# Expert tiles take turns in eight rooms; the router's weights and the first gather come earlier

## The chip, the cores and the metric

The kernel runs on one core of one Trainium2 chip. The time is the device time of one execution in microseconds. The reference takes one sequence of 256 tokens, 1024 features wide, all in float32.

## What is computed

The reference is a three-layer model; the change touches the second half of its first layer, the mixture of experts:

```python
x = x + g1[:, None, :] * y
h2 = modulate(x, norm2_g[l], sh2, sc2)
moe = hier_moe(h2.reshape(b * s, d), w_rg[l], b_rg[l], w_re[l], b_re[l],
               w1[l], w3[l], w2[l]).reshape(b, s, d)
x = x + g2[:, None, :] * moe
...
gp = softmax(h @ w_rg + b_rg);          g_w, g_idx = top_k(gp, 1)
el = (h @ w_re + b_re).reshape(t, 4, 8) # the 8 experts of the chosen group
e_w, e_loc = top_k(softmax(el_sel), 2)
weights = g_w * e_w / sum(e_w)
ys = (silu(xb @ w1[e]) * (xb @ w3[e])) @ w2[e]
```

There are 32 experts; a token goes to two of them. An expert has three weight tiles of [128 x 4096] float32 (2048 KB each): two with w1 and w3, one with w2. So 96 expert tiles are read whatever the routing. The layers behind it need the keys and values of a memory (256 rows by the matrices `w_kv`), which are computed in pieces beside the experts.

## The kernel before

Work is split in stages, each a block with one instruction stream per engine and a barrier of all engines at its end. All weights are read by SP, on one DMA queue, in the order in which SP issues them; SP waits on semaphores between the issues.

`stage_mix` (line 313) does attention, the recurrent mixer and the out projection. It streams the weight tiles named in `FRONT` through a ring of three slots, `ring`: tile n goes to slot n % 3 and is issued when tile n - 3 has been used (`tile(n)`, line 382). Between ring tiles SP also loads expert tiles that have buffers of their own: `expert0_0`, `expert0_1`, `expert0_2` for expert 0 (lines 406 to 414; the last two wait until the mixer no longer uses these buffers), and `early`, the first tile of expert 2. O0 and O1 are the two tiles of the out projection (PE line 560), A0 to A11 those of the adaptive modulation (line 287), M2 a tile of memory values kept in `mem_tile`. At the end of the stage PE turns the normed x by tokens (line 567), and DVE and ACT modulate it into `hT` (lines 998, 1006), the first half of the tokens in this stage, the second in the next.

`stage_route` (line 1029) loads the router's weights and bias row, the three ring slots with the tiles of expert 1, and two quarters of memory weights (`mem_part`, 512 KB each). PE computes the logits (line 1070), turns them and h back to tokens (lines 1086, 1076), does modulation tile A11 and, when DVE has chosen the experts, five small matmuls for the ranks (lines 1091 to 1095). DVE makes the combination weights while it waits for these. SP loads the row of the last norm (`norm_f`, line 1063) and waits for it before it leaves the stage.

`stage_experts` (line 1195) holds the accumulators in PSUM and goes through 16 pairs of experts. Each engine first reads the number of passes (here one). DVE makes the selection matrices for a pair (`select_pair`) and the weighted ones; PE gathers the tokens of a pair (`gather`, line 1286), DVE copies them to `x_gathered`. For an expert PE multiplies with tiles 0 and 1 (line 1339), does a piece of the memory's keys or values where one falls due (lines 1311, 1316), turns the weighted selection, scatters the expert before (line 1297), and multiplies with tile 2 (line 1364). Even experts use the `expert0` buffers, odd ones the ring's three slots; SP reloads a buffer when the tile in it has been used (line 1244), so seven tiles at most are in or on their way. A memory quarter is reloaded after both tiles and the last multiply of its expert. The pairs are in five code bodies: pairs 0 and 1 alone, 2 and 3, 4 to 7 and 8 to 15 as loops:

```python
SEGMENTS = ((0, 1, ("first", "keys0")), (1, 1, ("first", "keys0")), (2, 2, ("first", "keys0")),
            (4, 4, ("keys0", "keys1")), (8, 8, ("values", None)))
```

`stage_first_end` (line 1469) adds the result to x and norms it; the next layer (`tail`) streams its weights through the same ring.

## Time and profile before

| | us |
|---|---|
| median of 3 runs | 1506.67 (1505.97 to 1508.27) |
| the profiled execution | 1507.86 |
| its span | 1506.1 |
| PE busy | 1375.8 (91%) |
| PE's weight loads | 1042.6 (69%) |
| DVE, ACT, POOL busy | 656.4, 263.5, 229.2 |
| moved by DMA | 387.74 MB, mean 257 GB/s |

The stages in the profiled execution: the mixer to 221 us, the router to 247, the experts to 733, the rest behind.
### The profile page before, as it was taken

To read this page: it belongs to the slowest core of one execution; us is meant where nothing else is said; L and a number is where in the kernel's file an instruction comes from. 1 tells how busy PE (TensorE), PEld (TensorE's weight loads), DVE (VectorE), ACT (ScalarE), POOL (GpSimd) and SP (SyncE) were. 2 spreads that over 40 slices of the span, in tenths; PEclk is the share of its full clock that TensorE was granted. 3 is DMA by queue.
4 is the path that set the end of the run, shared out by engine and by line. 5 is a ranking of instruction groups with operands and counts; after the bars stand their busy time and mean duration, and the time that the engine had idled before them with its cause. 6 is when DMAs were issued, how large, how long until landed. Compare 5 with 4: busy or idle time off the path is not lost. (4 is left out here: it accounts for less than half of the span.)

```text
span 1506.1 us, 24580 instructions
## 1 busy us (share of the span) xinstructions
PE 1375.8 (91%) x10107; PEld 1042.6 (69%) x10107; DVE 656.4 (44%) x1235; ACT 263.5 (17%) x570; POOL 229.2 (15%) x227
## 2 busy tenths in 40 slices
PE   5999877998888888877899999999999999899998
PEld 2475434776556565555568788888887887788887
DVE  2545432111001110101353317376299999886573
ACT  2212111111101101100211022100233333330000
POOL 0000100000000000000166450099322122000000
PEclk9999996999989989988999999999999999999999
DMA  9637855999999999999743343556564444334441
GB/s 396 239 132 280 359 195 209 416 427 427 428 428 430 427 429 428 429 428 429 287 160 139 112 154 126 194 183 221 180 216 143 157 163 155 129 112 159 154 174 45
DMA packets 50797, 387.74 MB, mean 257 GB/s; under 512 B 6288, under 2 KB 21392, under 8 KB 29088
## 3 DMA queue, kind: packets, MB, share of 16 engines
q1 hardware_dynamic: 48128, 381.35, 64.0%
q10 hardware_dynamic: 2592, 5.31, 1.0%
q8 instruction: 54, 0.88, 0.2%
q14 instruction: 23, 0.19, 0.0%
HBM read 379.76 MB, written 6.88 MB: 257 GB/s over the span
## 5 line engine op out<-in xcount | busy, mean ns | idle before, releaser
L2551 PE MATMUL ps<-hT,ring 128*128 128x256 f32 x768 | 169.9, 381 | 1.0 <-PEq L1991 1.0
L2551 PEld LDWEIGHTS ps<-hT,ring 128*128 128x128 f32 x768 | 145.7, 192 | 20.3 <-issue 1.4
L1461 DVE TENSOR_TENSOR act_slots<-gate,ps 64x256 f32<-64x256 f32 x32 | 13.5, 423 | 241.0 <-ACT gate L1395 241.0
L1339 PE MATMUL ps<-expert,x_gathered 128*32 128x256 f32 x1024 | 72.4, 439 | 22.5 <-DMA expert<-in_experts 21.5
L1528 POOL TENSOR_SCALAR end_stat<-end_ss 128x1 f32<-128x1 f32 x2 | 0.9, 473 | 515.0 <-ACT expert L1518 514.9
L1339 PEld LDWEIGHTS ps<-expert,x_gathered 128*32 128x32 f32 x1024 | 36.2, 125 | 54.3 <-DMA expert<-in_experts 25.5
L1311 PE MATMUL ps<-memT,mem_part 128*128 128x256 f32 x192 | 53.7, 442 | 20.6 <-DMA mem_part<-in_mem_quarters 20.6
L267 PE MATMUL ps<-ring,hT 128*128 128x512 f32 x160 | 69.8, 594 | 0.0
L1286 PEld LDWEIGHTS ps<-sel,tokens 128*128 128x128 f32 x544 | 65.9, 200 | 5.0 <-issue 3.3
L1286 PE MATMUL ps<-sel,tokens 128*128 128x64 f32 x544 | 66.8, 284 | 0.4 <-DVE sel_weighted L1438 0.4
L1840 PE MATMUL ps<-ring,zT 128*128 128x256 f32 x288 | 66.9, 380 | 0.0
L1311 PEld LDWEIGHTS ps<-memT,mem_part 128*128 128x128 f32 x192 | 41.9, 224 | 32.9 <-DMA mem_part<-in_mem_quarters 23.9
L1339 PE MATMUL ps<-ring,x_gathered 128*32 128x256 f32 x1024 | 59.0, 380 | 2.0 <-DMA ring<-in_experts 2.0
L1840 PEld LDWEIGHTS ps<-ring,zT 128*128 128x128 f32 x288 | 54.6, 190 | 7.2
L1316 PE MATMUL ps<-mem_part,memT 128*128 128x128 f32 x256 | 42.0, 342 | 18.6 <-DMA mem_part<-in_mem_quarters 18.6
L1316 PEld LDWEIGHTS ps<-mem_part,memT 128*128 128x128 f32 x256 | 40.5, 253 | 23.9 <-DMA mem_part<-in_mem_quarters 23.9
L1463 DVE COPY x_gathered<-ps 128x512 f32<-128x512 f32 x16 | 11.1, 692 | 103.3 <-PE ps L1286 103.3
L2034 PE MATMUL ps<-hT,ring 128*128 128x256 f32 x256 | 55.7, 379 | 0.0
L267 PEld LDWEIGHTS ps<-ring,hT 128*128 128x128 f32 x160 | 30.0, 190 | 35.8 <-issue 35.8
L2659 POOL TENSOR_TENSOR ab_tmp<-b_raw,s_a_rows 128x256 f32<-128x256 f32 x32 | 28.0, 896 | 164.7 <-PE ps L2566 110.3
L2034 PEld LDWEIGHTS ps<-hT,ring 128*128 128x128 f32 x256 | 48.6, 190 | 6.4
L1438 DVE TENSOR_SCALAR sel_weighted<-const,rank,comb 128x128 f32<-128x128 f32 x66 | 19.9, 344 | 73.8 <-PE ps L1292 72.2
(651 smaller groups left out, 2523.0 us busy)
## 6 DMA issues: line engine op xcount, KB each, us to landing
ring<-in_weights SPq DMA_DIRECT2D x69, 2048.0 KB, 8.1
expert<-in_experts SPq DMA_DIRECT2D x48, 2048.0 KB, 22.3
ring<-in_experts SPq DMA_DIRECT2D x48, 2048.0 KB, 25.0
mem_part<-in_mem_quarters SPq DMA_DIRECT2D x20, 512.0 KB, 20.5
s_c_bar<-c_bar_out ACTq DMA_DIRECT2D x16, 256.0 KB, 2.4
c_bar<-s_c_bar SPq DMA_DIRECT2D x16, 256.0 KB, 2.7
mem_tile<-in_weights SPq DMA_DIRECT2D x1, 2048.0 KB, 21.7
b_raw<-in_s_b SPq DMA_DIRECT2D x16, 128.0 KB, 7.2
```

Source lines behind the costliest of these rows:

```text
L267: last = pe.matmul(bank, src[:, kk, h * P:(h + 1) * P], w[:, kk, :], start=(kk == 0), stop=(kk == KD - 1))
L1286: last = pe.matmul(xg_ps[:, f, :], a["tokens"][:, t, f * P:(f + 1) * P], sel[:, t].rearrange("p e s -> p (e s)"), start=(t == 0), stop=(t ...
L1311: last = pe.matmul(out, w[:, kk, :], k.memT[:, kk, :], start=(kk == 0), stop=(kk == KD - 1))
L1316: last = pe.matmul(out[:, h * P:(h + 1) * P], k.memT[:, kk, h * P:(h + 1) * P], cols, start=(kk == 0), stop=(kk == KD - 1))
L1339: last = pe.matmul(h_ps[group(g), :], xg[:, f, group(b)], w[:, kk, g, :], start=(f == 0), stop=(f == KD - 1))
L1438: last = dve.tensor_scalar(selw[:, b, t, :], k.c("iota32"), a["rank"][:, t, e], a["comb"][:, t, e], ALU.is_equal, ALU.mult)
L1461: dve.tensor_tensor(act_s[:], gate[:], h_ps[w3_out, :], ALU.mult).then_inc(act_ready, 1)
L1463: dve.tensor_copy(xg[:], xg_ps).then_inc(xg_ready, 1)
L1840: last = pe.matmul(self.sum_of(n, p), rows[:, kk, :], w[:, kk, :], start=(first and kk == 0 and self.PLACE[p][1] == 0), stop=(self.ends(i) ...
L2034: last = pe.matmul(bank[:, f, :], w[:, kk, (2 * h + f) * P:(2 * h + f + 1) * P], k.hT[:, kk, :], start=(kk == 0), stop=(kk == KD - 1))
L2551: last = pe.matmul(out[:, f, :], w[:, kk, (2 * h + f) * P:(2 * h + f + 1) * P], k.hT[:, kk, :], start=(kk == 0), stop=(kk == KD - 1))
L2659: pool.tensor_tensor(t_ab[:, c], b, bc(a_fm[:, q % 2, c, :], 1, 2), ALU.mult)
```

## The change

Expert tiles are numbered 0 to 95. Tile 0 goes to a room of its own, the buffer in which the memory's keys and values (`kmT`, `vm`) are put later; the others take turns in eight rooms. Tile n is issued when tile n - 8 has been used, in order. The eight are the three `expert0` buffers, one that was `early`, the three ring slots, and a new one, `late_room`, that exists from the router's stage on. Space comes from the memory quarters, which now go to `hT`, from the last norm's row, which goes to the row of `b_g1`, from the gate tiles, which go to `ada_part`, and from the mixer's `gate_quads` and `a_rows`, which go to a part of `expert0_1`.

```diff
+def room_of(k, a, n):
+    return [a["expert0"][0][:], a["room"][:], a["expert0"][1][:], a["expert0"][2][:], k.ring[:, 2, :], k.ring[:, 0, :],
+            a["late_room"][:] if "late_room" in a else None, k.ring[:, 1, :]][(n - 1) % N_ROOM] if n else a["kv"]
+
+def load_expert_tile(k, sp, a, n):
+    sp.dma_start(room_of(k, a, n), k.dram["experts"][n]).then_inc(room_landed(a, n), 16)
...
+                sp.dma_start(a["w_router"][:], d["w_router"]).then_inc(a["w_router_in"], 16)
+                at = ROWS["b_router"][0]
+                sp.dma_start(a["b_router"][:], d["rows"][at:at + 36].partition_broadcast(P)).then_inc(a["b_router_in"], 16)
                 for n in range(7, TILE_OF["A11"] + 1):
                     tile(n)
-                    if n == TILE_OF["VM"]:
-                        load_early(k, sp, a)
-                    if n == TILE_OF["A7"]:
-                        load_expert(k, sp, a, 0, 0)
-                    if n == TILE_OF["A9"]:
+                    if 7 <= n < 10:
+                        load_expert_tile(k, sp, a, n - 7)
+                    if n == TILE_OF["O0"]:
                         sp.wait_ge(pv_done, 4)
                         sp.wait_ge(silu_done, 2)
-                        load_expert(k, sp, a, 0, 1)
+                        sp.wait_ge(a_bc, 1)
+                        load_expert_tile(k, sp, a, 3)
                     if n == TILE_OF["A10"]:
                         sp.wait_ge(squares, 2)
-                        load_expert(k, sp, a, 0, 2)
+                        load_expert_tile(k, sp, a, 4)
...
                 turn_x(1)
+                pe.wait_ge(a["w_router_in"], 16)
+                pe.wait_ge(h_first_ready, 2)
+                logits_of(k, a, pe, 0)
```

The router's stage, SP:

```diff
-                sp.dma_start(w_router[:], k.dram["w_router"]).then_inc(router_in, 16)
-                at = ROWS["b_router"][0]
-                sp.dma_start(b_router[:], k.dram["rows"][at:at + 36].partition_broadcast(P)).then_inc(router_in, 16)
-                load_expert(k, sp, a, 1, TILE_OF["O1"] % RING)
-                load_expert(k, sp, a, 1, TILE_OF["A10"] % RING)
-                for b in range(2):
-                    load_part(k, sp, a, b, N_KEYS0 // 2 * (1 - b))
+                load_expert_tile(k, sp, a, 6)
+                load_expert_tile(k, sp, a, 7)
                 sp.wait_ge(k.tile_done, TILE_OF["A11"] + 1)
-                load_expert(k, sp, a, 1, TILE_OF["A11"] % RING)
+                load_expert_tile(k, sp, a, 5)
+                sp.wait_ge(h_turned, TT)
+                load_part(k, sp, a, 1)
+                load_expert_tile(k, sp, a, 8)
+                load_part(k, sp, a, 8)
                 at = ROWS["norm_f_g"][0]
-                sp.dma_start(a["norm_f"][:], k.dram["rows"][at:at + D].partition_broadcast(P)).then_inc(norm_f_in, 16)
-                sp.wait_ge(norm_f_in, 16)
+                sp.dma_start(a["norm_f"], k.dram["rows"][at:at + D].partition_broadcast(P)).then_inc(a["norm_f_in"], 16)
```

DVE waits for `norm_f_in` at the head of `stage_first_end` instead. In the router's stage ACT takes A11's part before it copies h; DVE computes ranks and `passes` first, then `select_pair`, then the combination weights and the late row of G11:

```diff
+                dve.drain()
+                select_pair(k, a, dve, lambda e: slice(e, e + 1)).then_inc(first_sel_ready, 1)
+                dve.wait_ge(exp_done, 1)
```

In the experts' stage SP is written out for all tiles, PE for twelve pairs (pairs 0 to 7, and a body of four that is gone through twice), and a memory quarter is reloaded after the first two tiles of its expert:

```diff
+                    for q in range(N_PAIR):
+                        for b in range(2):
+                            for j in range(3):
+                                load_next(p, 6 * q + 3 * b + j)
+                                if j == 1 and KINDS[q // 4][b] is not None:
+                                    load_next_part(p, part_of(q, b))
...
+                    for q0 in (0, 4):
+                        for r in range(4):
+                            pair(p, 0, q0 + r, KINDS[q0 // 4])
+                    with pe.Fori(0, 2) as i:
+                        for r in range(4):
+                            pair(p, i, 8 + r, KINDS[2])
...
-                for n in (T_END_FIRST, T_END_FIRST + 2, T_END_FIRST + 1):
-                    sp.wait_ge(done, n_pass * (3 * N_EXP) + (n % RING + 1 - 3 + DONE0))
+                for n, last in ((T_END_FIRST, 88), (T_END_FIRST + 1, 93), (T_END_FIRST + 2, 94)):
+                    sp.wait_ge(done, n_pass * N_TILE + (last + 1 - N_TILE + DONE0))
```

SP's issues in the second half of the mixer's stage, before (`ring` from `in_weights` are ring tiles 7 to 20, `in_experts` is the source of the expert tiles; `expert_0` is `early` the first time and `expert0_0` the second, since numbers inside a name are cut):

```order
L385 DMA ring<-in_weights 128x4096 x5
L1026 DMA expert_0<-in_experts 128x4096
L385 DMA ring<-in_weights 128x4096 x3
L1014 DMA expert_0<-in_experts 128x4096
L385 DMA ring<-in_weights 128x4096 x2
L1014 DMA expert_1<-in_experts 128x4096
L385 DMA ring<-in_weights 128x4096 x3
L1014 DMA expert_2<-in_experts 128x4096
L415 DMA mem_tile<-in_weights 128x4096
L385 DMA ring<-in_weights 128x4096
```

and now (from the router's weights on):

```order
L402 DMA w_router<-in_w_router 128x288
L404 DMA b_router<-in_rows 128x36
L385 DMA ring<-in_weights 128x4096
L1029 DMA kv<-in_experts 128x4096
L385 DMA ring<-in_weights 128x4096
L1029 DMA expert_0<-in_experts 128x4096
L385 DMA ring<-in_weights 128x4096
L1029 DMA expert_room<-in_experts 128x4096
L385 DMA ring<-in_weights 128x4096 x8
L1029 DMA expert_1<-in_experts 128x4096
L385 DMA ring<-in_weights 128x4096 x2
L1029 DMA expert_2<-in_experts 128x4096
```

Expert tiles 0, 1 and 2 now follow ring tiles 7, 8 and 9; `expert_1` is loaded after O0 (ring tile 17), where it was loaded before it, and the router's weights lead.

PE at the barrier between the mixer's stage and the router's (`UNCONDITIONAL_BRANCH` marks a stage's end and the next one's begin), before:

```order
L310 MATMUL ps<-ada_part,const 128x512
L567 MATMUL ps<-const,tokens 128x128 x8
L379 UNCONDITIONAL_BRANCH
L1066 UNCONDITIONAL_BRANCH
L1070 MATMUL ps<-hT,w_router 36x128 x16
L1076 MATMUL ps<-const,hT 128x128 x8
L1086 MATMUL ps<-const,logits_turned 128x36 x2
L1076 MATMUL ps<-const,hT 128x128 x8
```

and now:

```order
L310 MATMUL ps<-ada_part,const 128x512
L569 MATMUL ps<-const,tokens 128x128 x8
L1048 MATMUL ps<-hT,w_router 36x128 x8
L379 UNCONDITIONAL_BRANCH
L1112 UNCONDITIONAL_BRANCH
L287 MATMUL ps<-ring,crep 32x512 x8
L1048 MATMUL ps<-hT,w_router 36x128 x8
L1116 MATMUL ps<-const,hT 128x128 x8
```

Half of the logits (L1048, once L1070) stand ahead of the barrier now, and tile A11 (L287) stands ahead of the other half.

PE at the barrier between the router's stage and the experts', before:

```order
L1095 MATMUL ps<-chosen,const 128x32
L310 MATMUL ps<-ada_part,const 128x512
L1050 UNCONDITIONAL_BRANCH
L1279 UNCONDITIONAL_BRANCH
L1234 TENSOR_LOAD passes
L1234 ISA x2
L1372 MATMUL ps<-y,selT 128x512 x4
L1286 MATMUL ps<-sel,tokens 128x64 x16
```

and now:

```order
L1133 MATMUL ps<-chosen,const 128x32
L1134 MATMUL ps<-chosen,const 128x32
L1057 MATMUL ps<-sel,tokens 128x64 x16
L1098 UNCONDITIONAL_BRANCH
L1316 UNCONDITIONAL_BRANCH
L1276 TENSOR_LOAD passes
L1276 ISA x2
L1405 MATMUL ps<-y,selT 128x512 x4
```

The gather (L1057, once L1286) stands ahead of the barrier and of the load of `passes`; it stood behind them.

## Rows read from the trace of the kernel before

**Rows 1.** The page, the span in 40 slices of 37.65 us: GB/s.
```profile
GB/s 396 239 132 280 359 195 209 416 427 427 428 428 430 427 429 428 429 428 429 287 160 139 112 154 126 194 183 221 180 216 143 157 163 155 129 112 159 154 174 45
```

**Rows 2.** Stretches: length, busy us of each engine, granted clock, DMA share, GB/s.
```profile
201.00:212.00 11.00, 11.00 (x26) 4.96 (x27) 3.26 (x5) 1.44 (x4) 0.99 (x3) 1.00 0.01 1
...
246.00:262.00 16.00, 12.90 (x88) 9.41 (x92) 3.08 (x10) 1.28 (x1) 0.00 (x0) 0.52 0.04 8
...
282.00:726.00 444.00, 381.06 (x4465) 265.88 (x4464) 49.11 (x164) 47.94 (x141) 0.00 (x0) 0.92 1.00 425
```

**Rows 3.** Waits of PE, 255 to 780 us: sum, times, longest.
```profile
PE ps L1339 <- DMA expert<-in_experts: 21.5, 8, 3.0
PE ps L1311 <- DMA mem_part<-in_mem_quarters: 20.6, 5, 4.2
PE ps L1316 <- DMA mem_part<-in_mem_quarters: 18.6, 7, 2.8
...
PE ps L1339 <- DMA ring<-in_experts: 2.0, 4, 0.6
...
PE ps L1547 <- PEq L1236: 0.3, 1, 0.3
```

**Rows 4.** PE in order of time, third and fourth expert: start, length, instructions.
```profile
284.45 3.64 PE L1339 MATMUL ps<-expert,x_gathered 128*32 128x256 f32 x64
...
302.43 3.68 PE L1286 MATMUL ps<-sel,tokens 128*128 128x64 f32 x32
...
309.57 3.64 PE L1339 MATMUL ps<-expert,x_gathered 128*32 128x256 f32 x64
```

**Rows 5.** DMA in 255 to 275, 275 to 700, 700 to 760, 205 to 255.
```profile
expert<-in_experts SPq DMA_DIRECT2D x3, 2048.0 KB, 9.9
...
q8 instruction: 11, 0.18, 0.2%
...
ring<-in_experts SPq DMA_DIRECT2D x1, 2048.0 KB, 25.0
...
ring<-in_weights SPq DMA_DIRECT2D x1, 2048.0 KB, 8.1
...
norm_f<-in_rows SPq DMA_DIRECT2D x1, 512.0 KB, 9.2
```

**Rows 6.** PE in order of time around the out projection.
```profile
181.45 16.42 PE L560 MATMUL ps<-ring,mix_room 128*128 128x512 f32 x32 [4.55 <-DMA ring<-in_weights]
...
200.90 14.00 PE L560 MATMUL ps<-ring,mix_room 128*128 128x512 f32 x32 [1.32 <-DVE mix_room L968]
```

**Rows 7.** In order of time, router and first expert: one row of ACT, then PE.
```profile
221.38 1.50 ACT L998 ACTIVATE hT<-ps,mod 128x128 f32<-128x128 f32 x4 [2.35 <-PEq L379]
...
227.38 5.31 PE L1070 MATMUL ps<-hT,w_router 128*36 128x128 f32 x32 [6.30 <-DMA b_router<-in_rows]
...
239.45 0.41 PE L1091 MATMUL ps<-chosen,const 128*128 128x32 f32 x2 [2.62 <-DVE chosen L1163]
...
247.76 1.04 PE L1372 MATMUL ps<-y,selT 64*128 64x512 bf16 x4 [5.50 <-PEq L1050]
249.17 7.09 PE L1286 MATMUL ps<-sel,tokens 128*128 128x64 f32 x32 [0.37 <-DVE sel_weighted L1438]
257.23 5.73 PE L1339 MATMUL ps<-expert,x_gathered 128*32 128x256 f32 x64 [0.97 <-DVE x_gathered L1449]
```

**Rows 8.** SP's longest wait for a landing, 215 to 260, and two of its issues.
```profile
SPq L1050 <- DMA norm_f<-in_rows: 8.7, 1, 8.7
...
237.27 0.43 SPq L1063 DMA_DIRECT2D norm_f<-in_rows  x1
260.93 9.82 SPq L1244 DMA_DIRECT2D expert<-in_experts  x3
```

**Rows 9.** DVE in order of time, end of the router, start of the experts.
```profile
242.34 0.15 DVE L1192 TENSOR_SCALAR passes<-most 128x1 int32<-128x1 f32 x1
247.93 0.68 DVE L1432 TENSOR_SCALAR sel<-const,rank 128x32 f32<-128x32 f32 x4 [5.43 <-issue]
```

More of the change, by code:

```diff
@@ L518, in _ @@
                 for h in range(4):
-                    last = pe.matmul(abc[:, h, :], k.c("one_hot4")[0:4, h * P:(h + 1) * P], a_rows[:], start=True, stop=True)
+                    last = pe.matmul(abc[:, h, :], k.c("one_hot4")[0:4, h * P:(h + 1) * P], a_rows, start=True, stop=True)
                 last.then_inc(a_bc, 1)
@@ new lines, in logits_of, with gather @@
+def logits_of(k, a, pe, t):
+    for kk in range(KD):
+        last = pe.matmul(a["by_expert_ps"][:, t * P:(t + 1) * P], a["w_router"][:, kk, :], k.hT[:, kk, t * P:(t + 1) * P],
+                         start=(kk == 0), stop=(kk == KD - 1))
+    return last
+def gather(k, a, pe):
+    for f in range(KD):
+        for t in range(TT):
+            last = pe.matmul(a["xg_ps"][:, f, :], a["tokens"][:, t, f * P:(f + 1) * P],
+                             a["sel"][:, t].rearrange("p e s -> p (e s)"), start=(t == 0), stop=(t == TT - 1))
+    last.then_inc(a["xg_done"], 1)
@@ L1105, in _ @@
                 act_modulate(k, a, act, 1).then_inc(h_ready, 1)
+                act.wait_ge(*banks.full("A11"))
+                act.activation(a["part"][:], banks.bank("A11"), ACT.Copy).then_inc(banks.out("A11"), 1)
                 for t in range(TT):
@@ L1108, in _ @@
                     act.copy(h[:, t, :], a["turned_x"](t).rearrange("p f e -> p (f e)")).then_inc(h_copied, 1)
-                act.wait_ge(*banks.full("A11"))
-                act.activation(a["part"][:], banks.bank("A11"), ACT.Copy).then_inc(banks.out("A11"), 1)
                 act.wait_ge(gap_ready, 1)
@@ L1217, in stage_experts @@
         part_ps = k.ps[:, 7, TOK:2 * TOK]
-        N_SECOND = 8
-        SEGMENTS = ((0, 1, ("first", "keys0")), (1, 1, ("first", "keys0")), (2, 2, ("first", "keys0")), (4, 4, ("keys0", "keys1")),
-                    (8, 8, ("values", None)))
-        landed = a["expert_landed"]
-        rings = [[a["expert0"][j][:] for j in range(RING)], [k.ring[:, j, :] for j in range(RING)]]
+        KINDS = (("first", "keys0"), ("keys0", "keys1"), ("values", None), ("values", None))
+        part_of = lambda q, b: 2 * q + b if q < 8 else q + 8
@@ L1281, in _ @@
                 n_pass = passes(pe)
-                def gather():
-                    for f in range(KD):
-                        for t in range(TT):
-                            last = pe.matmul(xg_ps[:, f, :], a["tokens"][:, t, f * P:(f + 1) * P],
-                                             sel[:, t].rearrange("p e s -> p (e s)"), start=(t == 0), stop=(t == TT - 1))
-                    last.then_inc(xg_done, 1)
                 def turn_selection(b):
```

282 lines of the change are left out of this document (131 added, 151 removed).

## The prediction, made before the changed kernel was run

> **What bounds the kernel now.** I read the slices first, then stretches, then waits. The slices [rows 1] show DMA at 416 to 430 GB/s from slice 8 to slice 19. The stretches [rows 2] say it closer: nearly idle from 201 to 212 us (1 GB/s) and from 246 to 262 (8 GB/s), then busy without a gap from 282 to 726 (share 1.00, 425 GB/s), while PE is busy for 381 of those 444 us. So the expert stage is a stream of transfers that PE follows. The waits agree [rows 3]: PE waits for tiles or memory quarters for 21.5 + 20.6 + 18.6 + 2.0 = 62.7 us there, and for almost nothing else. A 2048 KB tile is 2.097 MB, at 428 GB/s 4.9 us; a memory quarter is 1.2 us. PE's own pace is quicker: two experts of the early kind take 309.57 - 284.45 = 25.1 us [rows 4], the stream needs 6 x 4.9 + 1.2 = 30.6.
>
> The end of the stage is therefore: the moment at which the stream runs for good, plus all bytes not yet carried, plus a short tail. At 257.23, when the first expert starts, 7 tiles and 2 quarters are in. The first three reloads are issued from 260.93 on, a median of 9.9 us before they land [rows 5], so the second lands near 275; 87 tiles and 18 quarters follow. Each microsecond that the stream starts earlier, and each tile that is carried in an idle stretch before it, comes off the end.
>
> **The change part by part.**
>
> *Two more rooms.* Tiles 0 to 8 are asked for before the stage, not seven. The idle stretches [rows 2] hold them: tiles 0 to 2 now go out behind ring loads between 52 and 82 us, where slices 2 and 3 moved only 239 and 132 GB/s. Two tiles less in the stream: 2 x 4.9 = **9.8 us**. First what the rows show: one core's reads run at 425 to 430 GB/s for over 400 us [rows 1, 2]. The Trainium skill ("DMA: Bandwidth & Descriptors", section Bandwidth) says that HBM to SBUF binds near 358 GB/s per core; by that rule a tile would take 5.9 us and this term would be 11.7. The trace disagrees with the rule, and 9.8 stands.
>
> *Out projection.* PE stood 4.55 us before it [rows 6], waiting for O0, which is queued behind expert 0's second tile. That tile now goes behind O0, so O0 lands about 181.4 - 4.9 = 176.5, when PE is ready (176.9). O1 still has one expert tile ahead and lands near 181.4 + 4.9 = 186.3. PE does its first 8 of 16 matmuls by 176.9 + 7.0 = 183.9 (half of the 14.00 us of the second block), waits, and ends near 186.3 + 7.0 = 193.3 instead of 197.87: **-4.6 us** for all that follows. Bounds: -3 if the clock falls in the remaining 2.4 us wait (it fell to 0.5 in the 4.55 us one, which is why this block took 16.42 and not 14.0), -4.9 if not even O1 is waited for.
>
> *Router.* PE waited 6.30 us for the bias row, then needed 5.31 for the logits [rows 7]. Both weights are now asked for at 31 us. Logits of the first half move ahead of the stage's barrier: half of the work, 1.8 us (of 5.31 with the clock down for most of it; 32 records of the gather take 3.68 at the full clock [rows 4], 16 of them 1.84). The second half needs the modulation of ACT and DVE, which starts only after that barrier: the turned x ends 227.38 - 6.30 - 4.6 = 216.5, logits to 218.3, barrier 0.3, modulation 1.5 (ACT's row [rows 7]; ada tile 11 lies beside it), logits 1.9: 222.0 against 232.69, so **-10.7 in all**. Cost of the moved logits: they hold back the modulation by 1.8, which is in this sum.
>
> *Gather in the router's stage.* From the logits' end, 232.69, to the ranking's first matmul it took 6.8 us [rows 7], and its five end 1.3 later. That stays: 230.1. DVE then ranks and selects at once, the ranks' four operations 0.8, their wait for PE 0.45, the four selections 0.68 [rows 9], PE's start 0.3: 2.2 us, so the gather begins at 232.3, with the weights computed beside it. It took 7.09 us at the half clock [rows 7] and 3.68 at the full one [rows 4]. I take 7.1: PE idled 2.6 us before the ranking, and the clock fell right after it (0.52 over 246 to 262 [rows 2, 7]); it ends at 239.4. The quick end is 236.0.
>
> *The barrier.* This is the part the diff hardly shows. SP waited 8.7 us for the final norm's row at the end of the router's stage [rows 8]; issued at 237.27 and 9.2 us to landing, it ended at 246.4, though DVE was done at 242.5 [rows 9]. PE went on at 247.76. The row is now awaited two stages later, so the stage ends with the gather, 239.4. From there 1.5 us to DVE's first instruction (247.93 - 246.4), then the copy of the gathered tokens, 0.97 from the gather's end to PE's first expert [rows 7]: the first expert starts at **241.9 instead of 257.2**. What is late next is the gather itself.
>
> *The stream.* Only tile 1's room is reloaded after the first two tiles, as tile 0's (the memory's room) is not reused, so reload one leaves about 5.8 us after the start (263.0 - 257.2, the end of tile 1) and reload two after tile 2, 13.2 us after the start before (the third of the x3 row of [rows 8], issued at 270.4), 12.5 here with fewer half-clock microseconds: 254.4, landing at 264.3 with the 9.9 of [rows 5]. The preloads are no obstacle: from 219 the queue carries four tiles, two quarters and the row, 4 x 4.9 + 3 x 1.2 + 3.3 latency = 26.5, done at 245.5. Before, reload two landed near 275.2: **10.9 us earlier, and after it 85 tiles and 18 quarters instead of 87 and 18: 9.8**. Sum 20.7.
>
> *More code.* Twelve bodies of a pair of experts are written out where five stood. The trace has 11 instruction fetches of 16 KB from 275 to 700 [rows 5], and the stream lost 3.4 us against its bare sum (425 against 428 GB/s over 444 us). I charge half of that again, 1.5 us; bounds 0 and 10. The register waits, the separate landing counters and the shared gate tile cost nothing while PE has 62 us of DMA waits to cover them. A quarter is now queued behind two tiles that are needed later; PE waits for them, but six loads stay issued behind it, so the stream doesn't stop.
>
> *Behind the stage.* The last tile landed 25.0 us after its issue at 700.9, at 725.9 [rows 5], and PE's multiply with it began 3.4 later; that multiply, the scatter and the barrier stay. The first tile of the next part lands directly behind it, and before it was on time too (PE waited 0.3 us there, for the barrier [rows 3]). Nothing is gained or lost.
>
> Sum: 20.7 - 1.5 = 19.2. The profiled execution took 1507.9 us (span 1506.1), the median of the runs is 1506.7, 1.2 below. 1506.7 - 19.2 = 1487.5; I say **1488**.
>
> **The rivals.**
> 1. *Full clock at the gather.* The shorter idle times keep the granted clock at 1.0. Gather and start come 3.4 earlier and the first tiles 1.4 faster: 24 to 25 us in all, 1482. For it: the 6.3 us wait is gone, after which the clock fell. Against: the 2.6 us idle ahead of the ranking is still there. Chance 0.2.
> 2. *The early start is not handed on.* The stream's head is thin: reloads one and two leave 8 us apart, and each waits for PE's first experts at a slow clock. If the start or the early quarters (ordered behind two tiles) bring only what the rooms do, 9.8 of 20.7 are left, less 1.5: 1498. The idle 246 to 262 speaks against it. Chance 0.15.
> 3. *Slower: instruction fetches.* PE's code for the stage goes from five bodies to twelve, and its last loop jumps back over four pairs. A fetch lies on the same 16 DMA engines; if each stalls a tile by 1.5 us, as the stream's 3.4 us loss allows for two of eleven, then 16 more fetches of that kind make 24 us and the time 1511. It decides from 13 such stalls on. The nearest row against it: 11 fetches lost 3.4 us together. The Trainium skill ("Runtime: NRT & Kernel Launch", Instruction fetch mechanics) says that a taken branch outside the window has to fetch its page before it goes on, which speaks against the long loop body and for the written out code. Chance 0.03.
> 4. *It doesn't do what it says.* If PE or the DMAs wait somewhere in the first stage for the new early tiles, the first gains vanish; the idle gaps of slices 2 to 4 [rows 1] leave no room for that. Chance 0.02, no change.
>
> **How the numbers follow.** My forecast has 0.6. Its own range is 1484 to 1492 (clock at the out projection, start of the stream, fetches 0 to 5). With rivals 1 and 2 inside, 1482 to 1497 holds 8 in 10 and more of what is left. A measurement tells 0.2%, 3 us, from no change. Faster takes the forecast, rivals 1 and 2: 0.95; same 0.02; slower 0.03.
>
> **What would show it.** Right: PE's wait ahead of the out projection under 3 us and at its middle; no wait at the logits; the gather before the barrier, from about 232; first expert near 242; the near idle stretch before the reloads under 5 us; last wait of the stage for a tile near 702, the last tile landing near 707; PE's DMA waits still about 60 us in sum, since start and end both move. Wrong: a first expert after 248, GB/s under 420 between 270 and 700, or a stage that ends less than 14 us earlier.

## The result and the profile after

| | before | changed |
|---|---|---|
| median | 1507.47 us (4 runs) | 1488.22 us (4 runs, 1485.48 to 1488.76) |
| profiled execution, span | 1507.86, 1506.1 | 1488.37, 1486.6 |
| ratio, 95% interval | | 0.9869 (0.9852 to 0.9886) |

The changed kernel is 19.3 us faster, and the forecast of 1488 holds. The sum behind it does not hold term by term, so the profile is read in the order of the prediction.

The page, the slices of 37.17 us, GB/s (before: [rows 1]):
```profile
GB/s 399 305 234 217 302 217 331 427 425 426 424 425 427 423 428 426 423 426 427 252 153 113 150 133 151 161 191 227 211 214 111 165 159 157 130 119 164 160 171 37
```
Slice 7 now carries 331 instead of 209. Stretches of the changed kernel: length, busy us of PE, PEld, DVE, ACT, POOL, granted clock, DMA share, GB/s:
```profile
246.00:262.00 16.00, 15.98 (x210) 10.55 (x203) 2.04 (x8) 2.04 (x6) 0.00 (x0) 0.94 0.60 219
282.00:706.00 424.00, 367.06 (x4236) 252.53 (x4228) 46.65 (x154) 48.27 (x136) 0.00 (x0) 0.91 1.01 426
265.96:711.34 445.38, 387.93 (x4502) 267.82 (x4501) 49.99 (x165) 52.24 (x145) 0.00 (x0) 0.91 1.01 426
711.34:737.08 25.74, 21.53 (x124) 10.97 (x123) 13.37 (x16) 6.69 (x13) 6.50 (x13) 1.00 0.57 228
737.08:1486.60 749.52, 727.20 (x4245) 618.69 (x4245) 485.53 (x784) 150.13 (x293) 211.08 (x192) 0.99 0.43 155
```
The first two rows answer to [rows 2]: from 246 to 262 us DMA has gone from 8 GB/s to 219, and the stream is as full as before. The other three cut the rest at the marks that the account below uses: landing of the second reload, landing of the last expert tile, first matmul of the next layer. The marks come from SP's issues and their times to landing, for example:
```profile
250.02 0.33 SPq L1029 DMA_DIRECT2D expert<-in_experts  x1
257.48 0.33 SPq L1029 DMA_DIRECT2D expert_room<-in_experts  x1
```
```profile
expert_room<-in_experts SPq DMA_DIRECT2D x1, 2048.0 KB, 8.5
...
late_room<-in_experts SPq DMA_DIRECT2D x1, 2048.0 KB, 37.4
```
The last row is the last expert tile, issued at 673.92 and landed at 711.34; the row above it is the second reload. PE around the out projection (before: [rows 6]) and from the logits to the first expert (before: [rows 7]):
```profile
177.03 7.11 PE L562 MATMUL ps<-ring,mix_room 128*128 128x512 f32 x16
186.72 8.72 PE L562 MATMUL ps<-ring,mix_room 128*128 128x512 f32 x16 [2.59 <-DMA ring<-in_weights]
...
218.59 1.94 PE L1048 MATMUL ps<-hT,w_router 128*36 128x128 f32 x16
...
222.68 1.94 PE L1048 MATMUL ps<-hT,w_router 128*36 128x128 f32 x16
...
231.38 0.64 PE L1130 MATMUL ps<-chosen,const 128*128 128x32 f32 x2 [3.61 <-DVE chosen L1204]
...
235.33 7.06 PE L1057 MATMUL ps<-sel,tokens 128*128 128x64 f32 x32 [1.61 <-DVE sel L1066]
243.60 1.04 PE L1405 MATMUL ps<-y,selT 64*128 64x512 bf16 x4 [1.21 <-PEq L1098]
244.69 3.53 PE L1373 MATMUL ps<-kv,x_gathered 128*32 128x256 f32 x32
```
The wait is at the projection's middle, the 6.30 us for the bias row are gone, the gather lies ahead of the barrier, and the barrier costs 1.21 us where it cost 5.50. PE's waits from 240 to 780 us (before: [rows 3]), sum, times, longest:
```profile
PE ps L1342 <- DMA hT<-in_mem_quarters: 22.8, 6, 6.0
PE ps L1373 <- DMA ring<-in_experts: 18.3, 7, 4.1
PE ps L1373 <- issue: 6.7, 2, 4.9
PE ps L1373 <- DMA expert_room<-in_experts: 4.2, 1, 4.2
PE ps L1373 <- DMA expert<-in_experts: 4.1, 3, 2.9
...
PE ps L1373 <- DMA late_room<-in_experts: 0.8, 1, 0.8
```
In sum these are 50.2 us for DMA. New are 6.7 us of "issue" in two waits, a stall for which no semaphore answers. Both stand at the start of the second trip of the loop over four pairs, where PE jumps back.

Where the 19.5 us between the two spans come from:

| part | before | changed | gain | forecast |
|---|---|---|---|---|
| up to the landing of the second reload | 275.23 | 265.96 | 9.3 | 10.9 |
| from there to the last expert tile | 450.67 (87 tiles) | 445.38 (85 tiles) | 5.3 | 9.8 - 1.5 = 8.3 |
| to the next layer's first matmul | 26.68 | 25.74 | 0.9 | 0 |
| from there to the end | 753.52 | 749.52 | 4.0 | 0 |

So two terms came out 4.6 us short together (1.6 and 3.0), and 4.9 us came from behind the last tile, 4.0 of them from the next layers, which the change does not touch. The experiments take the first two apart.

### The profile page after: what moved, and what is told of

Read it like the earlier page. It is cut to its first block and busy times, and to the rows that moved or that the text cites. A ratio compares the mean times of both kernels' runs of the same rounds, so it can differ in the third digit from the quotient of the medians.

```text
span 1486.6 us, 24369 instructions
## 1 busy us (share of the span) xinstructions
PE 1375.4 (93%) x10107; PEld 1039.3 (70%) x10107; DVE 656.5 (44%) x1235; ACT 267.3 (18%) x573; POOL 228.3 (15%) x227
## 5 line engine op out<-in xcount | busy, mean ns | idle before, releaser
L1470 DVE TENSOR_TENSOR ada_part<-ada_part,ps 64x256 f32<-64x256 f32 x32 | 13.5, 423 | 256.7 <-ACT ada_part L1426 256.7
L1057 PEld LDWEIGHTS ps<-sel,tokens 128*128 128x128 f32 x544 | 72.5, 217 | 6.9 <-issue 6.5
L1342 PE MATMUL ps<-memT,hT 128*128 128x256 f32 x192 | 55.2, 451 | 22.8 <-DMA hT<-in_mem_quarters 22.8
L1057 PE MATMUL ps<-sel,tokens 128*128 128x64 f32 x544 | 73.4, 301 | 1.6 <-DVE sel L1066 1.6
L1373 PE MATMUL ps<-ring,x_gathered 128*32 128x256 f32 x736 | 51.2, 428 | 23.2 <-DMA ring<-in_experts 18.3
L1342 PEld LDWEIGHTS ps<-memT,hT 128*128 128x128 f32 x192 | 43.0, 229 | 35.6 <-DMA hT<-in_mem_quarters 26.1
L1373 PEld LDWEIGHTS ps<-ring,x_gathered 128*32 128x32 f32 x736 | 25.3, 121 | 45.0 <-DMA ring<-in_experts 20.4
L1373 PE MATMUL ps<-expert,x_gathered 128*32 128x256 f32 x768 | 46.9, 390 | 5.9 <-DMA expert<-in_experts 4.1
L1327 PE MATMUL ps<-y,selT 32*128 32x256 f32 x528 | 48.9, 442 | 0.5 <-ACT y L1443 0.5
L1373 PEld LDWEIGHTS ps<-expert,x_gathered 128*32 128x32 f32 x768 | 25.1, 113 | 25.1 <-issue 5.8
```

The costliest lines, as they stand in the source:

```text
L1057: last = pe.matmul(a["xg_ps"][:, f, :], a["tokens"][:, t, f * P:(f + 1) * P], a["sel"][:, t].rearrange("p e s -> p (e s)"), start=(t == 0) ...
L1327: last = pe.matmul(acc(g, t), selT[group(g), b, t * P:(t + 1) * P], y[group(g), :], start=False, stop=stop, skip_group_check=True)
L1342: last = pe.matmul(out, w[:, kk, :], k.memT[:, kk, :], start=(kk == 0), stop=(kk == KD - 1))
L1373: last = pe.matmul(h_ps[group(g), :], xg[:, f, group(b)], w[:, kk, g, :], start=(f == 0), stop=(f == KD - 1))
L1470: dve.tensor_tensor(act_s, gate, h_ps[w3_out, :], ALU.mult).then_inc(act_ready, 1)
```

## The experiments

Ratios are to the kernel before on the same chip (1506.98 us for kernels 1 to 4, 1506.38 for 5 to 8, 1506.49 for 9 to 12). The changed kernel itself was not run beside them. Differences below are of medians; since the kernel before was 0.5 to 1.1 us quicker beside them than beside the changed kernel, the ratios put every variant up to 2 us higher against the changed kernel. A difference of 2 to 4 us from the changed kernel can therefore be told from no change only where the trace shows it too.

| kernel | us (runs) | ratio, 95% interval |
|---|---|---|
| 1 changed, norm row awaited in the router's stage | 1495.70 (6) | 0.993 (0.9916 to 0.9943) |
| 2 before, norm row not awaited there | 1503.58 (12) | 0.9981 (0.9972 to 0.999) |
| 3 changed, gather behind the barrier | 1490.72 (5) | 0.9897 (0.9884 to 0.991) |
| 4 changed, router's weights late | 1493.45 (6) | 0.992 (0.9902 to 0.9939) |
| 5 before, PE's pairs written out | 1509.51 (11) | 1.002 (1.0011 to 1.0029) |
| 6 changed, six rooms | 1497.99 (5) | 0.9943 (0.9929 to 0.9956) |
| 7 six rooms, short loops | 1493.35 (5) | 0.9913 (0.99 to 0.9927) |
| 8 changed, five extra matmuls | 1487.73 (4) | 0.9871 (0.9856 to 0.9886) |
| 9 changed, eight rooms then six, short loops | 1486.04 (4) | 0.9863 (0.9844 to 0.9882) |
| 10 changed, tile 3 behind O1 | 1485.06 (5) | 0.9855 (0.9837 to 0.9873) |
| 11 changed, seven extra matmuls | 1484.50 (5) | 0.9854 (0.9832 to 0.9875) |
| 12 changed, 9 + 10 + 11 | 1473.91 (5) | 0.9786 (0.9769 to 0.9803) |

One caution for reading single traces: in the kernels whose program is the same up to the out projection (the changed one and 1, 3, 6 to 12), its first matmul came anywhere from 174.43 to 177.60. What one trace says of the start is therefore counted from that matmul. First expert, counted so: changed 67.66, kernel 1 73.39, 3 71.46, 4 71.83, 6 67.60, 8 66.60, 9 67.47, 10 62.48, 11 63.15, 12 58.92.

**1 and 2. The barrier.** In the changed kernel the wait put back, and in the one before the same wait moved to its user:
```diff
+                sp.wait_ge(a["norm_f_in"], 16)          # kernel 1, after SP's issue of the row
-                sp.wait_ge(norm_f_in, 16)               # kernel 2, at the same place
+                dve.wait_ge(a["norm_f_in"], 16)         # kernel 2, at the head of stage_first_end
```

> The changed kernel with one line back: SP waits for the last norm's row at the end of the router's stage. If that wait is a price of its own, the stage ends when the row lands, 248.3 in the changed kernel, instead of with the gather, 242.4; the first expert starts near 250.6 instead of 244.7, the stream's first reload as much later, and the time is 6 us (5 to 7.5) above the changed kernel's. If the early start is hidden by PE's slack of some 60 us anyway (rival), less than 1 us.

> The kernel before with that wait alone moved: DVE waits for the row at the head of the stage behind the experts. The router's stage should end with DVE, 242.5, instead of 246.4: first expert near 253.3 and 4 us less than before (3 to 5). The rival, that the start of the experts is hidden, gives no difference.

The longest wait of SP in kernel 1, then PE at the start of the experts in kernel 1 and, last two rows, in kernel 2:
```profile
SPq L1098 <- DMA rows_b_g<-in_rows: 19.3, 1, 19.3
```
```profile
235.82 7.06 PE L1057 MATMUL ps<-sel,tokens 128*128 128x64 f32 x32 [1.60 <-DVE sel L1066]
249.99 1.04 PE L1406 MATMUL ps<-y,selT 64*128 64x512 bf16 x4 [7.11 <-issue]
```
```profile
241.61 1.04 PE L1372 MATMUL ps<-y,selT 64*128 64x512 bf16 x4 [2.00 <-PEq L1050]
251.08 5.35 PE L1339 MATMUL ps<-expert,x_gathered 128*32 128x256 f32 x48 [0.97 <-DVE x_gathered L1449]
```
Kernel 1 gives 7.5 us back by the medians, where 5 to 7.5 was expected; its first expert is 5.7 us later. Kernel 2 gains 3.4 with that line alone: PE waits 2.00 us at the barrier instead of 5.50 [rows 7]. The barrier is shown from both sides, and it is worth twice as much behind the early gather as without it, because the other work is then done earlier: SP waits 19.3 us for the row in kernel 1, and waited 8.7 before [rows 8].

**3 and 4. The gather and the router's weights**, each put back alone:
```diff
-                pe.wait_ge(h_copied, TT)                # kernel 3, in the router's stage
-                pe.wait_ge(first_sel_ready, 1)
-                gather(k, a, pe)
+                gather(k, a, pe)                        # kernel 3, behind the barrier
...
-                sp.dma_start(a["w_router"][:], ...)     # kernel 4: weights, bias row and all logits
-                logits_of(k, a, pe, 0)                  # go back to the router's stage
```

> The changed kernel with the first gather back behind the barrier. The router's stage ends with DVE near 238.2, the barrier, the load of passes and the four small matmuls come first, then 7.1 us of gather: first expert near 248.5 against 244.7, time 4 us (3 to 5) above the changed kernel's. If only the barrier's end counted, it would be faster, not slower.

> The changed kernel with the router's weights loaded in the router's stage again and all logits there. They take 5.6 us to land, ahead of the expert tiles in the queue, and both halves of the logits follow: logits end near 231 instead of 224.5, first expert near 250 to 251, time 5 to 7 us above the changed kernel's. Rival: the wait is hidden behind DVE's and ACT's modulation, 2 us.

The first expert is 3.8 us later (kernel 3) and 4.2 us later (kernel 4), where about 4 and 6 were expected. In time kernel 3 loses 2.5 us by the medians and 4.2 by the ratios (3 to 5 expected), kernel 4 5.2 and 7.7 (5 to 7 expected). Kernel 3 does not give back the whole 7.06 us of the gather, since PE then stands at the barrier while DVE ends its work for the router:
```profile
237.97 1.04 PE L1402 MATMUL ps<-y,selT 64*128 64x512 bf16 x4 [5.61 <-PEq L1098]
238.93 7.09 PE L1057 MATMUL ps<-sel,tokens 128*128 128x64 f32 x32
```
In kernel 4 PE waits 2.72 us for the bias row, not 6.30 as before, so the weights' early load is worth less beside the other parts than it was in the sum.

**5, 6 and 7. Rooms and code.**
```diff
...
-                            with pe.Fori(0, count) as i:        # kernel 5
-                                pair(p, i, off, parts)
+                        for i in range(count):
+                            pair(p, 0, off + i, parts)
...
-N_ROOM = 8                                                      # kernels 6 and 7
+N_ROOM = 6
...
-                    for q0 in (0, 4):                           # kernel 7
-                        for r in range(4):
-                            pair(p, 0, q0 + r, KINDS[q0 // 4])
-                    with pe.Fori(0, 2) as i:
-                        for r in range(4):
-                            pair(p, i, 8 + r, KINDS[2])
+                    for r in range(4):
+                        pair(p, 0, r, KINDS[0])
+                    with pe.Fori(0, 4) as i:
+                        pair(p, i, 4, KINDS[1], 1)
+                    with pe.Fori(0, 4) as i:
+                        for r in range(2):
+                            pair(p, i, 8 + r, KINDS[2], 2)
```

> The kernel before, with TensorE's sixteen pairs of experts all written out in place of five bodies in loops of one pair. No transfer and no arithmetic differs; only more pages of code are fetched while the stream runs. Theory (a fetch on the saturated DMA engines costs the stream about 0.15 to 0.2 us each, since the change lost 8.0 us with about 41 fetches where the kernel before lost 3.4 with about 12): about 28 more fetches, last tile landing 4 to 5 us later, time 4.5 us longer (bounds 3 to 6). Rival (what the changed stream lost is its order of transfers or its thinner start, not the fetches): the same time within 1 us. Second rival (a jump back of a loop costs more than the fetches): 1 to 3 us shorter.

> The changed kernel with six rooms in place of eight: tiles 7 and 8 are no longer asked for ahead of the stage, all else stays. Theory (every tile that is carried before the stage comes off the end of the stream): last tile landing and time 9.8 us later, near 1498 (bounds 9 to 11). Rival (the DMA idles after the barrier anyway, because reload one waits for tile 1's room: two tiles less would end the preloads 9.8 us sooner and only widen an idle stretch, so the whole 9.8 is lost, and with a thinner head the stream runs dry at the early experts as well): 12 us or more. Second rival (the rooms' gain is given back later): under 6 us.

> As the one with six rooms, but TensorE's pairs four to seven in a loop of one pair and pairs eight to fifteen in a loop of two pairs (four trips each), so that the loop bodies are short enough not to be fetched again. About 18 fetches in the stream instead of 41. Theory (fetches cost the stream 0.15 to 0.2 us each): 3 to 5 us faster than with six rooms and the long loop, near 1494.5, and no wait of 4.9 us at a jump back. Rival (the fetches are hidden, the loss is something else): the same as with six rooms within 1 us, near 1498. Second rival (each jump back costs TensorE time that the stage's end sees): 1 to 3 us slower.

The stretch from the landing of the second reload to that of the last tile in kernel 6 and in kernel 7, and from their two pages the queue that fetches instructions (packets, MB, share):
```profile
263.42:718.65 455.23, 384.34 (x4502) 259.76 (x4501) 49.97 (x165) 52.18 (x145) 0.00 (x0) 0.93 1.01 425
```
```profile
264.31:715.03 450.72, 372.34 (x4486) 252.55 (x4486) 49.98 (x165) 52.18 (x145) 0.00 (x0) 0.96 1.01 427
```
```profile
q8 instruction: 83, 1.36, 0.4%
```
```profile
q8 instruction: 59, 0.97, 0.3%
```
Kernel 7 moves the same bytes of weights with 24 fetches less, and needs 4.5 us less in this stretch and 4.6 us less by the medians. The other kernels agree:

| stretch | kernel, fetches in the whole trace | of them in the stretch | us |
|---|---|---|---|
| 87 tiles, 18 quarters | before, 54 | 11 | 450.67 |
| | 5, 80 | 37 | 454.43 |
| | 6, 83 | 38 | 455.23 |
| | 7, 59 | 15 | 450.72 |
| 85 tiles, 18 quarters | changed, 83 | 38 | 445.38 |
| | 9, 59 | 15 | 441.17 |
| | 10 and 11, 83 | 38 | 445.65, 446.14 |
| | 12, 59 | 15 | 441.02 |

26 fetches more cost kernel 5 3.8 us in this stretch and 3.1 us of time, where 4.5 was expected. (Its profiled execution is the slowest of its eleven, 1514.27 us; 2.7 us of that lie ahead of the stretch.) 23 fewer save 4.5 (7 against 6) and 4.2 (9 against changed). That is 0.14 to 0.20 us for each, where its 16 KB at 428 GB/s would be 0.04. PE waits for DMA in all of them, so it is the stream that gets longer. How a fetch costs more than its bytes is not shown: by the share that the page gives, the packets of 38 fetches took 0.6% of the sixteen DMA engines' time in this stretch and those of 11 took 0.2%, a difference of 1.8 us of the 4.6. And two rooms are worth 455.23 - 445.38 = 9.85 us in the stretch, the 9.8 of the forecast. The rival that six rooms starve the stream is out: the DMA share of kernel 6 is 1.01 too.

The jump back costs PE itself something. In the changed kernel and in kernel 6, at the second trip of the loop over four pairs (first row of each); kernels 7 and 9 have no such row:
```profile
605.29 3.64 PE L1373 MATMUL ps<-ring,x_gathered 128*32 128x256 f32 x32 [4.90 <-issue]
610.72 3.64 PE L1373 MATMUL ps<-expert,x_gathered 128*32 128x256 f32 x32 [1.78 <-issue]
```
```profile
612.45 3.62 PE L1370 MATMUL ps<-ring,x_gathered 128*32 128x256 f32 x27 [4.49 <-issue]
```
The Trainium skill ("Runtime: NRT & Kernel Launch", Instruction fetch mechanics) says that a taken branch out of the pages at hand has to fetch its target first; the trace agrees. Here the stall can hide in the slack that PE has against the stream. Kernel 5 has the fetches without a jump back. At its price, 0.145 us, the 23 fetches that kernels 7 and 9 save make 3.3 us of their 4.5 and 4.2, so about 1 us is left that may be the jump's; no run shows that it is.

**8 and 11. The clock at the gather.** Matmuls whose result nobody reads, between the logits and the ranking and between the ranking and the gather; three and two of them in kernel 8, four and three in kernel 11:
```diff
+                for _ in range(4):
+                    pe.matmul(banks.bank("A11"), k.c("quarters"), a["part"][:], start=True, stop=True)
                 pe.wait_ge(chosen_ready, 1)
...
+                for _ in range(3):
+                    pe.matmul(banks.bank("A11")[:, 0:256], k.c("quarters"), a["part"][:, 0:256], start=True, stop=True)
                 pe.wait_ge(h_copied, TT)
```

> The changed kernel with five extra matmuls whose results nobody reads: three of 512 columns while TensorE waits for the chosen weights, two of 256 ahead of the gather. Theory (rival 1 of the prediction: the granted clock fell to 0.5 because TensorE idled 3.6 us before the ranking): the clock stays at 1.0 through ranking and gather; ranking 1 us shorter, gather 3.7 instead of 7.06 us, first expert near 240.5 instead of 244.7, the first three tiles also quicker; reload two lands 4 to 6 us earlier, time 4 to 6 us shorter, near 1483. Rival (the preloads still run until 248, so an earlier first expert and earlier reloads only queue behind them): gather shorter but reload two at most 2 us earlier, time within 2 us of the changed kernel. Second rival (the clock falls all the same, and the extra matmuls delay the ranking): 0 to 1.5 us slower.

> As the one with five extra matmuls, with seven: four of 512 columns ahead of the ranking, three of 256 ahead of the gather, so that TensorE has almost no idle time from the logits to the gather. Theory (idle time ahead of the gather lets the clock fall, and with five extra matmuls 1.04 and 0.66 us of it were left): granted clock 1.0 to the gather's end, gather 3.7 us instead of 6.92, first expert 3 us earlier than with five, time 1 to 3 us below the changed kernel (the preloads run until 243 to 248 and bound what the first reload can win). Rival (the clock falls at the gather whatever TensorE did before, as it did with five): gather 6.9 to 7.1 us again, same time as the changed kernel within 1 us or slower by up to 1.

Kernel 8, PE in order of time, then two stretches (the clock is the third number from the end):
```profile
229.56 0.41 PE L1132 MATMUL ps<-chosen,const 128*128 128x32 f32 x2 [1.04 <-DVE chosen L1208]
...
232.47 6.92 PE L1057 MATMUL ps<-sel,tokens 128*128 128x64 f32 x32 [0.66 <-DVE sel L1066]
```
```profile
231.00:232.00 1.00, 0.81 (x4) 0.38 (x2) 0.85 (x7) 0.00 (x0) 0.00 (x0) 1.00 1.18 508
...
233.00:235.00 2.00, 2.00 (x11) 2.00 (x11) 1.70 (x9) 0.00 (x0) 0.00 (x0) 0.50 1.07 459
```
Kernel 11, the same:
```profile
231.34 0.41 PE L1132 MATMUL ps<-chosen,const 128*128 128x32 f32 x2 [0.18 <-DVE chosen L1208]
...
234.25 3.76 PE L1057 MATMUL ps<-sel,tokens 128*128 128x64 f32 x32 [0.23 <-DVE sel L1066]
```
```profile
236.00:240.00 4.00, 2.62 (x22) 1.99 (x21) 1.57 (x4) 0.50 (x1) 0.00 (x0) 1.00 1.01 426
```
With five extra matmuls the ranking ran at 2.4 GHz (five matmuls 0.22 us apart instead of 0.43), but the clock fell to 1.2 GHz as the gather began, after idle times of 1.04 and 0.66 us. The median is 0.5 us below the changed kernel's, no difference, where 4 to 6 us were expected; the clock fell all the same, as the second rival says. With seven, and idle times of 0.18 and 0.23, it stayed at 2.4 GHz and the gather took 3.76 us, in kernel 11 and again in kernel 12. The first expert of kernel 11 is 3.5 us earlier than with five (3 expected) and 4.5 us earlier than in the changed kernel. Its median is 3.7 us lower, where 1 to 3 was expected, with the intervals of the two ratios overlapping. The Trainium skill ("TensorE: Matmul & The Clock Gate", Part 1) says that the gate follows how busy the engine has been lately; the trace agrees.

The idle time right ahead does not by itself say when the clock falls. The changed kernel idled 3.61 us before the ranking and ran all of it at half clock. Kernel 10 idled 3.63 us there, and its first three matmuls still took 0.39 to 0.41 us each, as at the full clock; the last took 0.62, as at half, and then came the gather at half (7.06 us):
```profile
224.65 0.41 PE L1130 MATMUL ps<-chosen,const 128*128 128x32 f32 x2 [3.63 <-DVE chosen L1204]
...
225.62 0.62 PE L1134 MATMUL ps<-chosen,const 128*128 128x32 f32 x2
```

**9. Eight rooms, then six.** From tile 24 on the rooms of tiles 7 and 8 are left out of the rotation, so that loops of one and of two pairs are possible again:
```diff
+LAST_EIGHT = 24
+def room_index(n):
+    return (n - 1) % N_ROOM if n < LAST_EIGHT else n % 6
```

> The changed kernel with nine tiles ahead of the stage in eight rooms as now, but from tile 24 on only six of the rooms take turns, so that TensorE's pairs four to seven can be a loop of one pair and pairs eight to fifteen a loop of two, as in the experiment with six rooms and short loops. Theory (fetches of code are what the changed stream loses, 0.15 to 0.2 us each, and two rooms are worth 9.8 us only because two tiles more are carried early): about 59 fetches instead of 83, time 4 to 5 us below the changed kernel, near 1484. Rival (the deeper backlog of eight rooms is needed in steady state as well): the stream runs dry somewhere after tile 24, and the time is above 1488.

The last tile lands 5.2 us earlier than in the changed kernel, 4.2 of it from the stretch in the table. The median is 2.2 lower, where 4 to 5 was expected, and the intervals overlap, so by the time alone this one is not told from the changed kernel; its profiled execution gave 3.3 us back behind the experts (752.84 against 749.52, the same code). The rival, that the deeper backlog is needed in steady state, is out.

**10. The wait in the out projection.** Expert tile 3 behind O1:
```diff
-                    if n == TILE_OF["O0"]:
+                    if n == TILE_OF["O1"]:
                         sp.wait_ge(pv_done, 4)
```

> The changed kernel with expert tile 3 asked for behind O1 instead of between O0 and O1. Theory (the 2.6 us wait in the middle of the output projection is for O1 behind that tile, and the clock fell in it): O1 lands near 181, 5 us earlier, no wait and no half clock in the projection, which ends 4.3 us earlier, and all up to the end of the stage follows, since the DMA is nearly idle from 201 to 220 anyway: time 4 us below the changed kernel, near 1484 (bounds 3 to 4.5). Rival (the preloads then hold up the early stage instead: tiles and quarters are asked for later relative to their use): under 2 us. Second rival (the next layer of waits, A10 or the modulation, takes it back): no change.

```profile
174.73 13.97 PE L562 MATMUL ps<-ring,mix_room 128*128 128x512 f32 x32
...
237.21 2.87 PE L1373 MATMUL ps<-kv,x_gathered 128*32 128x256 f32 x32
```
No wait, no half clock: 13.97 us from the first to the last matmul, where the changed kernel needed 195.44 - 177.03 = 18.4. The first expert is 5.2 us earlier and the median 3.2 lower, where 3 to 4.5 was expected (the intervals overlap again). Its profiled execution, like that of kernel 11, lost 6.3 us around the last tile (32.08 us from its landing to the next layer instead of 25.74): for a part of it the clock was at half, and the last gather took 7.09 us instead of 3.79.
```profile
703.49:735.57 32.08, 27.87 (x139) 15.63 (x138) 13.38 (x16) 6.69 (x13) 6.50 (x13) 0.84 0.45 178
```

**12. All three.**

> The three together: six of the eight rooms in rotation from tile 24 on with short loops, expert tile 3 behind O1, and the seven extra matmuls. If the parts add up as the single runs are expected to (4.5, 4 and 1 to 3 us below the changed kernel): 1477 to 1480. If only the loops and O1 hold: near 1480. If one of them eats another's gain (an earlier start of the stage meets preloads that are not done): 1482 to 1484.

PE in kernel 12 and its stretch from the second reload to the last tile:
```profile
227.84 3.76 PE L1076 MATMUL ps<-sel,tokens 128*128 128x64 f32 x32 [0.23 <-DVE sel L1085]
232.81 1.04 PE L1425 MATMUL ps<-y,selT 64*128 64x512 bf16 x4 [1.21 <-PEq L1117]
233.91 2.89 PE L1393 MATMUL ps<-kv,x_gathered 128*32 128x256 f32 x32
```
```profile
254.49:695.51 441.02, 397.67 (x4502) 274.81 (x4501) 50.01 (x165) 52.20 (x145) 0.00 (x0) 0.90 1.01 427
```
It takes 1473.91 us, 32.6 below before and 14.3 below the changed kernel (12.5 by the ratios): the fastest here, and below the expected 1477 to 1480. The parts nearly add up in the trace: first expert 8.7 us earlier (5.2 + 4.5 = 9.7 singly), the stream 4.4 shorter, 13.1 together. The fear that preloads not yet done would eat the earlier start did not come true. The medians of 9, 10 and 11 (2.2, 3.2 and 3.7, sum 9.1) had said less; in at least one execution of each, half-clock stretches behind the experts took part of the gain back.

## Why the prediction was right

The time came out as forecast, and part of that is luck: two terms were 4.6 us too large together, and 4.9 us that the sum had at nothing made up for them. The mechanism, an earlier start of a stream that then runs full and has two tiles less to carry, is what the traces show.

*Two more rooms, 9.8*: 9.85 us in the stream between kernel 6 and the changed one, and 9.8 us between their medians. Right. The prediction sets the trace against a limit of 358 GB/s from the Trainium skill ("DMA: Bandwidth & Descriptors", section Bandwidth) and says that they disagree. The same section of the Trainium skill gives about 358 GB/s for each of two cores that stream together, and 425 GB/s measured for one core alone. This kernel runs on one core, and the 426 GB/s of its trace agrees.

*Out projection, -4.6*: it ended at 195.4 instead of 197.87, so -2.4. The wait at its middle came as forecast (2.59 us, O1 at 186.7 where 186.3 was forecast), but the clock fell behind it and the second half took 8.72 us, not 7.0. The text had this as its bound, -3, and chose the other value. The 2.59 us of wait are one expert tile's place in the queue: with tile 3 behind O1, kernel 10 has neither the wait nor the half clock.

*Router*: the forecast was 6.1 of its own beside the 4.6. The logits ended at 224.62 against 232.69, 8.1 earlier, 2.4 of it from the projection: 5.7. Right.

*From logits to gather*: forecast 10.3 us, measured 224.62 to 235.33, 10.7. Two errors of about 1 us cancel: the clock fell already at the ranking, whose matmuls took 2.3 us and not 1.3, and DVE needed less ahead of the gather (1.61 against 2.2). The gather at the half clock, 7.1: 7.06.

*Barrier and first expert*: 2.5 us from the gather's end forecast, 2.3 measured, so 244.69 is 2.8 later than 241.9 for the items above, 2.2 of it for the out projection. That SP's wait for the norm row is what held the stage is shown by kernels 1 and 2.

*The stream's start, -10.9*: -9.3. Of the 2.8 us lost above 1.1 came back, since the second reload landed 8.5 us after its issue and not 9.9: nothing was queued ahead of it. That is the thin head of rival 2, as a small term: preloads were done at 248.3, the first reload was issued at 250.02, the second 7.5 us later.

*More code, 1.5*: 4.6 us, the largest miss among the terms that the change moves. The step that failed is its price. Half of the 3.4 us that the stream had lost against its bare sum was charged again, as if the number of fetches grew by half (425 against 428 GB/s over 444 us is 3.1 us, so the 3.4 is a slip of its own). The number went from 11 to 38 in the stretch (54 to 83 in the trace); that is what it would be if each of the 16 pairs is now fetched, those of the last loop's second trip too. At 3.4 us for 11 fetches the same row would have given 8.3 for 27 more, more than the 4.6 measured; the step that was missing is a count of the pages. Rival 3 had the mechanism and a price some ten times too high: 1.5 us a fetch against 0.14 to 0.20.

*Behind the stage, 0*: -0.9 and -4.0 in the profiled pair. No instruction of the next layers differs. The kernel before, to be set beside the changed one's last stretch above:
```profile
752.58:1506.10 753.52, 730.30 (x4245) 621.29 (x4245) 485.40 (x784) 150.30 (x293) 212.03 (x192) 0.98 0.44 154
```
Their first 16 matmuls took 8.80 us before and 7.11 after, for the clock alone. In the records of the granted clock this part stood at half for 24.7 us before and for 18.7 after; those 6.0 us are 3.0 us of work at the full clock, so 1 us of the 4.0 is not placed. From the next layer's first matmul to the end the three traces made from the kernel before (before, 2, 5) needed 753.4 to 753.7 us, the eleven made from the changed one 749.2 to 752.8, depending on where half-clock stretches fell: kernel 9, whose first 16 matmuls also took 8.80 us, needed 752.8. So the 4.6 us short in front were made up by 4.9 us from behind, of which 4.0 are a part that the change leaves alone and which the sum had at nothing. Why the half-clock stretches fall otherwise in the kernels made from the changed one is open; no run was made for it.

*Rival 1 (full clock at the gather)* did not happen, and kernel 11 shows why: the idle times, not the wait for the bias row alone. It priced the case at 24 to 25 us in all, so 5 more than the forecast; kernel 11 measured 3.7. *Rivals 2 and 4* did not decide.

Of the signs that were named: PE's wait ahead of the projection (2.59, at its middle), no wait at the logits and the gather before the barrier came as written. The near idle stretch before the reloads came too (0 GB/s from 248 to 250 us). The first expert was at 244.69 instead of 242, PE's last wait for a tile ended at 706.49 instead of near 702, the last tile landed at 711.34 instead of 707. The DMA waits were 50 instead of 60 us; PE now also stands 6.7 us for its own code, which may be part of that.

## What to carry to other kernels

Where one stream of transfers sets the end, count what it must carry once it runs for good, then ask what starts it: a wait of the issuing engine for a transfer that nobody in the next stage needs can hold the whole barrier, here for 3.4 us in one kernel and 7.5 in the other. Count code as traffic of the same stream: each 16 KB fetch cost 0.14 to 0.20 us here, so a rotation of buffers should have a period that lets the loop bodies stay short. And when a short matmul burst stands behind a chain on another engine, idle time ahead of it can cost more than it seems: here five filler matmuls kept the clock only to the burst's start and won nothing, two more made the burst 3.3 us shorter than the changed kernel's. Last, a total that comes out right does not vouch for its terms: here 4.6 us of misses were hidden by 4.9 us from another place.

## What the runs showed of the hardware that was not expected

- A fetch of 16 KB of instructions costs a saturated stream four to five times the time of its bytes (0.14 to 0.20 us against 0.04).
- The clock fell to 1.2 GHz at the gather after idle times as short as 1.04 and 0.66 us (one trace); with 0.18 and 0.23 it stayed at 2.4 GHz (two traces). After the same 3.6 us of idle time the ranking ran at half clock in one kernel and began at the full clock in another.
- A jump back over four pairs stalled PE for 4.90 and 1.78 us; loops of one or two pairs showed no such wait.
- The same instructions brought the first matmul of the out projection at 174.43 to 177.60 us, a scatter as large as some of the effects looked for.
